# The triangular inverse of block 2's recurrence as two 64x64 blocks per head, two chunks in flight, and its finish and the merge as one phase

## The reference

```python
def rwkv7_mix(p, ...):                      # 8 heads of 64
    def step(state, inp):
        r_t, d_t, k_t, v_t, kk_t, a_t = inp
        sa = jnp.einsum('bhij,bhj->bhi', state, -kk_t)
        state = (state * d_t[:, :, None, :] + sa[..., None] * (kk_t * a_t)[:, :, None, :]
                 + v_t[..., None] * k_t[:, :, None, :])
        return state, jnp.einsum('bhij,bhj->bhi', state, r_t)
    ...
    y = (y - mean) * lax.rsqrt(var + LNX_EPS)      # per head
    y = y * lnx_g + lnx_b
    return (y + bonus) * g                  # g = sigmoid(gd) @ g_up
...
g_a, g_b = jnp.split(jax.nn.sigmoid(p_gate), 2, axis=-1)
merged = g_a * (y_a @ w_o_rwkv) + g_b * (y_b @ w_o_att)
```

## Time and profile before

| | |
|---|---|
| median of 3 runs | 2798.94 us (2798.93 to 2804.11) |
| the profiled execution | 2801.4 us, its span 2799.7 us, mean TensorE clock 0.956 |
| PE busy in the span | 2625.1 us, 94% |
| chain of waits | PE 83%, DVE 11% |
| recurrence (`rwkv_scan`), from its first to the next phase's first matmul | 1949.6 to 2195.1 us |
| `rwkv_finish` | 2195.1 to 2233.1 us |
| `merge` | 2233.1 to about 2370 us |

### The profile page before, as it was taken

How to read it: one execution, slowest core, us unless ns; L and a number is a source line. 1 busy time by engine, 2 the same in 40 slices (tenths; PEclk the granted TensorE clock), 3 DMA queues, 4 the chain that set the end, 5 groups by cost and what they waited for, 6 DMA issues and landing times.

```text
span 2799.7 us, 32246 instructions
## 1 busy us (share of the span) xinstructions
PE 2625.1 (94%) x13098; PEld 2133.2 (76%) x13098; DVE 1097.3 (39%) x1755; ACT 550.9 (20%) x1111; POOL 1525.5 (54%) x1419
## 2 busy tenths in 40 slices
PE   8998998999999998999999899686999798999998
PEld 6778876888888885588888786454888487888887
DVE  3353856352242203345133448745544312411023
ACT  1112312020020116712011122234222111110010
POOL 7545564497684863348677555410332366576664
PEclk9997999999999999999999989897999799999999
DMA  5212032242231320023232131200000132233221
GB/s 162 75 54 61 1 106 76 66 134 94 84 111 69 113 98 15 1 83 113 90 98 98 49 98 46 68 23 0 1 1 1 49 90 91 76 106 98 90 83 68
DMA packets 104280, 198.89 MB, mean 71 GB/s; under 512 B 9306, under 2 KB 12612, under 8 KB 104132
## 3 DMA queue, kind: packets, MB, share of 16 engines
q1 hardware_dynamic: 101476, 189.36, 21.1%
q10 hardware_dynamic: 2656, 7.47, 0.7%
HBM read 194.71 MB, written 2.10 MB: 70 GB/s over the span
## 4 chain that ended last, share of the span: by engine, by line
PE 83%; DVE 11%; ACT 1%; POOL 1%; issue 1%; SPq 0%; DVEq 0%; DMA 0%; POOLq 0%; ACTq 0%
PE psum L153 33%; PE psum L293 22%; PE psum L155 7%; PE psum L232 3%; PE psum L2038 2%; PE psum L2048 1%; PE psum L1256 1%; PE psum L1247 1%; PE psum L1275 1%; POOL weight_split_ring L412 1%; DVE big L1809 1%; PE psum L964 1%; DVE best L1808 1%; DVE big L869 1%; PE psum L194 1%
## 5 line engine op out<-in xcount | busy, mean ns | idle before, releaser
L412 POOL TENSOR_TENSOR weight_split_ring<-weight_ring,weight_split_ring 128x512 fp32r<-128x512 f32 (+2 forms) x732 | 954.3, 1325 | 30.5
L153 PE MATMUL psum<-x_split,weight_split_ring 128*128 128x512 f32 x4080 | 955.9, 395 | 13.6 <-DVEq L2671 13.1
L153 PEld LDWEIGHTS psum<-x_split,weight_split_ring 128*128 128x128 f32 x4080 | 771.3, 190 | 180.6 <-DVEq L2671 13.3
L409 POOL TENSOR_SCALAR weight_split_ring<-weight_ring 128x1024 fp32r<-128x1024 f32 (+2 forms) x366 | 394.7, 1078 | 790.8 <-PE psum L293 340.5
L293 PE MATMUL psum<-weight_split_ring,hidden_split 128*128 128x512 f32 x2448 | 577.3, 397 | 8.2 <-DVEq L2671 8.2
L293 PEld LDWEIGHTS psum<-weight_split_ring,hidden_split 128*128 128x128 f32 x2448 | 460.9, 189 | 120.2 <-DVEq L2671 8.6
L155 PE MATMUL psum<-weight_split_ring,x_split 128*128 128x512 f32 (+2 forms) x1056 | 240.4, 388 | 2.0 <-DVEq L2671 1.4
L155 PEld LDWEIGHTS psum<-weight_split_ring,x_split 128*128 128x128 f32 x1056 | 197.0, 207 | 44.4 <-issue 7.2
L704 DVE TENSOR_TENSOR big<-big 128x512 f32<-128x512 f32 x64 | 88.9, 1389 | 178.5 <-ACT big L689 178.5
L2181 POOL TENSOR_TENSOR big<-big,pair_masks 128x512 f32<-128x512 f32 x48 | 60.9, 1272 | 153.7 <-PE psum L2038 94.7
L511 DVE SCALAR_TENSOR_TENSOR residual<-residual,psum 128x512 f32<-128x512 f32 x48 | 32.8, 683 | 262.6 <-PE psum L293 262.6
(11 more groups left out here) (340 smaller groups left out, 2839.3 us busy)
## 6 DMA issues: line engine op xcount, KB each, us to landing
weight_ring<-in_mlp_w SPq DMA_DIRECT2D x128, 512.0 KB, 3.5
weight_ring<-in_w_in SPq DMA_DIRECT2D x92, 512.0 KB, 3.6
weight_ring<-in_w_ffn_in SPq DMA_DIRECT2D x40, 512.0 KB, 3.4
weight_ring<-in_w_out SPq DMA_DIRECT2D x24, 512.0 KB, 3.6
weight_ring<-in_w_ffn_out SPq DMA_DIRECT2D x22, 512.0 KB, 3.8
weight_ring<-in_sb_w_q SPq DMA_DIRECT2D x8, 512.0 KB, 3.6
weight_ring<-in_sb_w_k SPq DMA_DIRECT2D x8, 512.0 KB, 3.6
weight_ring<-in_sb_w_v SPq DMA_DIRECT2D x8, 512.0 KB, 3.6
```

The lines of the kernel that those rows point to most:

```text
L153: mm = pe.matmul(out, wp[:, k, m * P:(m + 1) * P], xp, start=first, stop=last)
L409: pool.tensor_scalar(part.high[:, 0:nk, 0:n], raw, 1.0, 0.0, ALU.mult, ALU.add).then_inc(self.high_made, 1)
L412: low = pool.tensor_tensor(part.low[:, k, 0:n], raw[:, k, :], part.high[:, k, 0:n].bitcast(F32), ALU.subtract)
```

## The change

1. Per head and chunk the inverse is kept as two 64x64 diagonal blocks (rows h = 0, 1 of 64 tokens) and one far block. A tile holds 8 heads by 64 columns (`Xc`, `Yc`, `U`, `level`, `kb`, `farL`), the first diagonal block on partitions 0-63 and the second on 64-127. Levels 1 to 5 work on both with 64x64x64 products; level 6 is the far block alone. DVE writes it, and ACT the two diagonal blocks (`diagonal`), into the full X that `mixes` and `state_reads` use. The turn of X is now a product with the identity (L2099), and ACT copies it, no more DVE.
2. Two chunks are in flight. Stage k holds `turn`, `near`, `far`, `pairs` and levels 1 to 3 of chunk k, and between them levels 4 to 6, `mixes`, `state_reads`, `new_state` and `outputs` of chunk k-1. There are five stages.
3. `pairs` makes three kinds instead of five, 128x128, and now takes g = 0 and g = 1 in turn into different banks; `new_state` and `outputs` take the groups in turn too.
4. `rwkv_finish` and `merge` are one phase, `finish_merge`. The first two gate projections run through 4 banks between the finish's products, the other 4 banks serve the finish. The output gate is copied by ACT; the bias `lnx_b` is added to the bonus by ACT, and scale and sum are one DVE instruction.
5. Some semaphores of `second_front` are joined, POOL cuts three more pieces of masks at setup, and the tiles' places in memory differ (more of the split buffers is used).

The near products and a level on PE (`rows(h)` is partitions 64h to 64h+63):

```diff
+            for n, left, right in ((0, kap, bet), (1, bet, kap)):
                 for q in range(NHP):
...
-        def level(c, lv):
+                    for h in range(2):
+                        for g in range(2):
+                            mm = pe.matmul(near_half(c, n)[rows(h), g, q], left(g, q, block(c, h)),
+                                           right(g, q, block(c, h)), start=True, stop=True)
...
+        def level_u(c, lv):
+            s, bank = c % 2, level_banks(c)[0]
+            pe.wait_ge(s_xu[s], version(c, lv - 1))
+            if lv < LAST:
+                pe.wait_ge(s_lm[s], mask(c, lv))
+                for u in range(HEADS):
+                    for h in range(2):
+                        mm = pe.matmul(by_head(bank)[rows(h), u], m.level[s][rows(h), u, :], m.Xc[s][rows(h), u, :],
+                                       start=True, stop=True)
+            else:
+                pe.wait_ge(s_fc, c + 1)
+                for u in range(HEADS):
+                    mm = pe.matmul(by_head(bank)[rows(0), u], m.farL[s][rows(1), u, :], m.Xc[s][rows(1), u, :],
+                                   start=True, stop=True)
+            mm.then_inc(s_u[s], 1)
+        def level_x(c, lv):
+            s, bank = c % 2, level_banks(c)[1]
+            pe.wait_ge(s_uc[s], product(c, lv))
+            pe.wait_ge(s_yu[s], version(c, lv - 1))
+            for u in range(HEADS):
+                for h in range(2 if lv < LAST else 1):
+                    mm = pe.matmul(by_head(bank)[rows(h), u], m.Yc[s][rows(h), u, :], m.U[s][rows(h), u, :],
+                                   start=True, stop=True)
+            mm.then_inc(s_dx[s], 1)
+        def level_y(c, lv):
+            s, bank = c % 2, level_banks(c)[1]
+            pe.wait_ge(s_xu[s], version(c, lv))
+            for u in range(HEADS):
+                for h in range(2):
+                    mm = pe.matmul(by_head(bank)[rows(h), u], m.Xc[s][rows(h), u, :], m.ident[rows(h), rows(h)],
+                                   start=True, stop=True)
+            mm.then_inc(s_yt[s], 1)
```

Stage k on PE:

```diff
+        for k in range(NT + 1):
+            new, old = k < NT, k >= 1
+            if new:
+                turn(k)
+            if old:
+                level_u(k - 1, 4)
+            if new:
+                near(k)
+                far(k)
+            if old:
+                level_x(k - 1, 4)
+            if new:
+                pairs(k, 0)
+            if old:
+                level_y(k - 1, 4)
+            if new:
+                level_u(k, 1)
+            if old:
+                level_u(k - 1, 5)
+            if new:
+                pairs(k, 1)
+                level_x(k, 1)
+            if old:
+                level_x(k - 1, 5)
+            if new:
+                level_y(k, 1)
+            if old:
+                level_y(k - 1, 5)
+            if new:
+                pairs(k, 2)
+                level_u(k, 2)
+            if old:
+                level_u(k - 1, 6)
+            if new:
+                level_x(k, 2)
+            if old:
+                level_x(k - 1, 6)
+            if new:
+                level_y(k, 2)
+            if old:
+                mixes(k - 1)
+            if new:
+                level_u(k, 3)
+            if old:
+                state_reads(k - 1)
+            if new:
+                level_x(k, 3)
+            if old:
+                new_state(k - 1)
+            if new:
+                level_y(k, 3)
+            if old:
+                outputs(k - 1)
```

The near products on DVE, which before were done per group and with other masks:

```diff
+        def near(c):
+            s = c % 2
+            dve.wait_ge(s_ne, 2 * c + 1)
+            if c >= 2:
+                dve.wait_ge(s_lm[s], mask(c, 0))
+            kb, x, y = groups(m.kb[s]), groups(m.Xc[s]), groups(m.Yc[s])
+            dve.tensor_copy(kb, near_half(c, 0)).then_inc(s_kb, 1)
+            dve.wait_ge(s_kb, c + 1)
+            step(dve.tensor_tensor(y, kb, cut_near(1), ALU.mult))
+            dve.tensor_tensor(y, cut_near(7), y, ALU.subtract).then_inc(s_yu[s], 1)
+            if c >= 2:
+                dve.wait_ge(s_xf, c - 1)
+            step(dve.tensor_tensor(x, near_half(c, 1), cut_near(0), ALU.mult))
+            dve.tensor_tensor(x, cut_near(7), x, ALU.subtract).then_inc(s_xu[s], 1)
```

The finish on PE:

```diff
+        gates = itertools.chain(*(g.stream(pe, m.x_tile) for g in plan[0][:2]))
+        def go_on(n):
+            for _ in range(n):
+                next(gates)
+        def sums(t):
+            if t >= 3:
+                pe.wait_ge(s_cen, t - 2)
+            pe.matmul(bank(t), m.halves[:, :], m.yaF[:, t, :], start=True, stop=True).then_inc(s_fp, 1)
+        for t in range(3):
+            sums(t)
+        go_on(1)
+        sums(3)
+        go_on(3)
+        for t in range(NHP):
+            pe.wait_ge(s_bo, t + 1)
+            if t < 3:
+                pe.wait_ge(s_cen, t + 2)
+            else:
+                pe.wait_ge(s_bv, t - 2)
+            pe.matmul(bank(4 + t), m.halves[:, :], m.bonus[:, t, :], start=True, stop=True).then_inc(s_fp, 1)
+            go_on(1)
+        for t in range(NHP):
+            pe.wait_ge(s_sq, t + 1)
+            head_sums(kit, m, pe, 4, t, m.ysqF).then_inc(s_fp, 1)
+            go_on(1)
+        pe.wait_ge(s_up, 16)
+        for t in range(NHP):
+            if t < 3:
+                pe.wait_ge(s_bv, t + 2)
+            else:
+                pe.wait_ge(s_gr, t - 2)
+            pe.matmul(bank(8 + t), m.g_up[:, t * P:(t + 1) * P], m.rwF[:, 13, :], start=True, stop=True).then_inc(s_fp, 1)
+            go_on(1)
+        go_on(2)
+        pe.wait_ge(s_inv, 1)
+        for t in range(NHP):
+            if t < 3:
+                pe.wait_ge(s_gr, t + 2)
+            else:
+                pe.wait_ge(s_nr, t - 2)
+            spread_heads(kit, m, pe, 5 + (12 + t) % 3, t).then_inc(s_fp, 1)
+            go_on(2)
+        go_on(6)
```

More of the change, by code:

```diff
@@ new lines, in scalar @@
+        for k in range(NT + 1):
+            new, old = k < NT, k >= 1
+            if new:
+                copies(k)
+            if old:
+                level_u(k - 1, 4)
+            if new:
+                far(k)
+            if old:
+                level_y(k - 1, 4)
+            if new:
+                level_u(k, 1)
+            if old:
+                level_u(k - 1, 5)
+            if new:
+                level_y(k, 1)
+            if old:
+                level_y(k - 1, 5)
+            if new:
+                level_u(k, 2)
+            if old:
+                level_u(k - 1, 6)
+                diagonal(k - 1)
+            if new:
+                level_y(k, 2)
+            if old:
+                mixes(k - 1)
+            if new:
+                level_u(k, 3)
+            if old:
+                corrections(k - 1)
+            if new:
+                level_y(k, 3)
+            if old:
+                outputs(k - 1)
@@ L2338, in merge @@
-def merge(nc, kit, m, a):
+        for k in range(NT + 1):
+            new, old = k < NT, k >= 1
+            if new:
+                near(k)
+            if old:
+                level_x(k - 1, 4)
+            if new:
+                pairs(k, 0)
+                level_x(k, 1)
+            if old:
+                level_x(k - 1, 5)
+            if new:
+                pairs(k, 1)
+                level_x(k, 2)
+            if old:
+                level_x(k - 1, 6)
+            if new:
+                pairs(k, 2)
+                level_x(k, 3)
+            if 1 <= k < NT:
+                new_state(k - 1)
@@ L2370, in scalar @@
+        for j in range(PARTS):
+            if j >= 1:
+                for n in range(8):
+                    gate(j, n)
             for n in range(4):
```

614 lines of the change are left out of this document (311 added, 303 removed).

## The result

The changed kernel takes 2719.5 us (median of 4 runs, 2718.66 to 2720.62) against 2798.96 (2798.93 to 2804.11): ratio 0.9712, 95% interval 0.9695 to 0.9729. That is 79.5 us less where the forecast had 60, and inside the forecast's range.

What follows compares the result with a forecast made beforehand. PE's work was taken as the bound. From 2801.4 us, savings of 50.5 in the recurrence (245.5 to 195) and 10 in finish and merge (173 to 163) gave 2741 profiled, 2739 median; range 2706 to 2796, likeliest case to 2775.

Steps and rivals of the forecast that it cites:

- the halves run side by side: Levels 1 to 5: products of h = 0 and h = 1 in turn overlap, 0.029 us a record instead of 0.058.
- Rival A: Levels 1 to 5: the halves do not overlap in one bank, 56 us more, 2795 us; chance 0.10.
- Rival B: U4 to X3 of stages 1 to 3: the clock stays at its lower level, 2807 us; chance 0.12.
- Groups: Levels: a group of 32 records of 64x64x64 products takes 0.93 us, 1.0 with its start.
- The wait before Y4: Middle stage: PE waits 2.6 us for X4's update on DVE, behind the near products' five instructions.
- Stages 1, 2 and 3: Recurrence: 37, 44 and 44 us, with 3.5 us for the clock in each of the 44s.
- Stage 0 has one chunk alone and starts, as now, at half clock: First stage of the recurrence: 34 us, or 27 at full clock.
- stage 4: Last stage of the recurrence: 29 to 30 us, 36 with half clock in the reads and outputs.
- Near: Near products of a middle stage: 64 records at 0.029, 1.9 us; four-way overlap at 0.015 only in the lower end.
- One wait appears: a gate projection now has 4 banks ... four times: Finish: the second projection's first tile waits for ACT to read the first's; with one table load, 7.3 us.
- The 2.6 us for changes between fp32 and gate products: Finish: some twenty changes between the two kinds of product on PE at 0.13 us each, 2.6 us.
- POOL's first chunk: Start of the finish: no wait, one chunk takes POOL 3.8 us and PE has the first sums to do.

Runs made afterwards that it cites:

- e2: Changed kernel, but each level group takes all h = 0 products and then all h = 1 instead of the halves in turn: 2854.9 us.
- the three edits: On the changed kernel, in order: U4 ahead of the turn (2709.8 us alone), state reads grouped by shape (2704.4), outputs' state products at the end (2721.4).
- e12: Changed kernel with U4 ahead of the turn and state reads grouped by shape, one start a bank, outputs as in the changed kernel: 2688.2 us.
- e10: Changed kernel with U4 ahead of the turn, state reads grouped by shape and outputs' state products at the end, one start a bank: 2680.0 us.
- e9: Changed kernel with only the outputs altered: the 16 state products at the group's end, one start a bank: 2721.4 us.

## Why the prediction was right, and where it was off

**Direction and mechanism.** That PE's stream is the bound and that the halves run side by side was right, and both were tested. The rule of the Trainium skill, TensorEngine Tiling (Array Packing), Restrictions and Gotchas, that row tiles cannot use one bank at the same time, does not hold for a level's two halves, which lie in different partitions of one bank: 0.034 us a record in turn, 0.055 apart. The measurement decides for this case; no two row tiles of the new recurrence write the same partitions of one bank, so that case stays open. Rival A fell by this. Rival B fell for the changed kernel (0.89 and 0.88 in the middle stages), but its mechanism is real: e2 shows it.

**The recurrence, 185.0 against 195.** Groups: 1.08 against 1.0, 60 of them, 5 us too little. The wait before Y4: 3.01 against 2.6. State reads 6.4 (with their part at half clock) against 5.8. Stages 1, 2 and 3: 35.3, 45.7, 44.3 against 37, 44, 44. The step that failed by more is "Stage 0 has one chunk alone and starts, as now, at half clock": 34 took all of it at half clock, while the window has 0.78; 28.6 measured; PE was at half clock for 12.6 of these and from 1964.5 on at full clock. And stage 4: 36 against 31.0; its levels took 12.1 us (2102.43 to 2114.53) for my 13.9, and half clock set in only in the middle of the state reads and ended before the outputs did (2121.5 to 2131.8). A drop behind the new 3.0 us wait was not in the forecast. That the middle stages came so near their 44 is in part luck: fifteen full groups at 1.08 make 1.2 us more than I had, the near products 0.9 less, and the clock cost 5.0 and 5.3 (the missing share of the two stages) for my 3.5.

**Near** cost 1.0 (0.015 x 64) instead of 1.9: I used two halves side by side, and four quarters ran; this was the 3 us that the lower end had for it.

**Finish and merge, 153.2 against 163.** Here a step was wrong, not only a size: "One wait appears: a gate projection now has 4 banks ... four times". PE and ACT at that place, both of the changed kernel:

```profile
2137.61 1.65 PE L153 MATMUL psum<-x_split,weight_split_ring 128*128 128x512 f32 x6 [1.32 <-POOL weight_split_ring L412]
...
2162.18 1.02 PE L2499 MATMUL psum<-big,gain_rows 128*128 128x512 f32 x2
...
2164.44 1.02 PE L2499 MATMUL psum<-big,gain_rows 128*128 128x512 f32 x2
...
2186.93 11.17 PE L153 MATMUL psum<-x_split,weight_split_ring 128*128 128x512 f32 x48
2197.95 2.27 PE L153 MATMUL psum<-hidden_split,weight_split_ring 128*128 128x512 f32 x9
```

```profile
2163.86 1.28 ACT L2529 ACT_TABLE_LOAD   x1
2165.15 0.60 ACT L2529 ACTIVATE big<-psum 128x512 f32<-128x512 f32 x1
...
2171.38 0.60 ACT L2529 ACTIVATE big<-psum 128x512 f32<-128x512 f32 x1 [0.78 <-PE psum L153]
```

PE does one gate step behind each product of the output gate, 2.26 us apart (2162.18, 2164.44), and so the four tiles of the first projection end 2.26 us apart too. ACT reads the first at 2165.15 and the last at 2171.38, while the second projection returns to each bank only four steps after its tile ended. The wait that I priced at 7.3 us had several us of slack, even with the table load (1.28) in it. The 2.6 us for changes between fp32 and gate products did not appear either: a gate record is 0.230 (48 from 2186.93 to 2197.95), six are 1.38, and 0.88 of the period of 2.26 is left for the fp32 product, under the 0.93 it costs alone. Against this PE did wait 1.3 us for POOL's first chunk, which I had called no wait.

## What to carry to other kernels

Price a small fp32 product by where its neighbour lies: two products in different quarters of the array overlapped here (0.034 us a record), two in the same quarter did not (0.055), and a loop's order decides which it is. Do not add up the gains of removing waits and of joining products of one shape one at a time: here the three edits alone gave 13.1, 13.3 and 0.8 us of the recurrence and together 37.0. The first two together gave 27.3, about their sum; with the third the half clock in stage 4 went too (17 us of it in e12, none in e10), though the third edit alone did not take it away (20 us of it in e9). Before pricing a bank wait, write down when the tile ended and when its bank is used next, step by step.

## What the hardware showed that I had not expected

- Four quarters of the array in turn: 0.015 us a record of 64x64x64, against 0.034 in two and 0.055 in one.
- The clock: with all levels in one quarter at a time it was at 1.2 GHz most of the time (0.57 over 322 us) although PE was busy for 301 of these; with the halves in turn it held 2.4 GHz for 35 us on end in stage 1.
- Passing between 128-row and 64-row products every two records doubled the time of the state reads, 5.8 us at full clock (0.36 for two records) against 2.97 in two blocks. That is 0.18 a passage.
